# Keys' and values' block compression: two weight products of one 64-column half of the array each, one after the other or side by side

## The reference, cut to what matters

```python
def compress_blocks(t, w1, w2, pos):
    blk = t[:, idx] + pos[None, None, :, None, :]
    blk = jnp.moveaxis(blk, 3, 1).reshape(B, G, n_cmp, CMP_BLOCK * dh)
    return jax.nn.gelu(blk @ w1) @ w2
...
kc = compress_blocks(k_c, cmp_k_w1, cmp_k_w2, cmp_k_pos)
kc = rms_norm(kc, nsa_k_g)
vc = compress_blocks(v_c, cmp_v_w1, cmp_v_w2, cmp_v_pos)
```

## Time and profile before, and how to read it

| | us |
|---|---|
| median of 3 runs | 1147.88 |
| lowest and highest run | 1144.9, 1153.52 |
| the profiled execution | 1147.36 |
| its span (first to last instruction) | 1145.6 |
| its mean granted TensorE clock | 0.966 |

### The profile page before, as it was taken

One profiled execution on the slowest core, in us unless ns is written; L12 is line 12 of the kernel. 1 busy time (PEld: TensorE's weight loads), 2 busy tenths in 40 slices (PEclk: granted clock), 3 DMA queues, 4 the chain that ended last, 5 costly groups with the idle time before them and its releaser, 6 DMA issues.

```text
span 1145.6 us, 16492 instructions
## 1 busy us (share of the span) xinstructions
PE 1048.0 (91%) x6109; PEld 896.9 (78%) x6109; DVE 850.4 (74%) x1665; ACT 654.4 (57%) x1312; POOL 45.6 (4%) x44
## 2 busy tenths in 40 slices
PE   4898999896899999999988999799997999889997
PEld 4776878786687887888767989688875888878875
DVE  4677866674599999999968676697657877668674
ACT  5453645543688888887844576532445377642342
POOL 0201100000101001010000000000101000000010
PEclk9999999996899999999999999899998999889999
DMA  8432333341399999999944333332344433313320
GB/s 332 164 110 79 142 148 148 111 184 37 116 386 352 388 367 353 376 362 365 367 172 177 142 116 111 110 111 111 133 179 152 150 122 143 116 74 111 114 108 37
DMA packets 30036, 211.32 MB, mean 184 GB/s; under 512 B 3584, under 2 KB 3712, under 8 KB 4992
## 3 DMA queue, kind: packets, MB, share of 16 engines
q1 hardware_dynamic: 28368, 205.01, 48.3%
q10 hardware_dynamic: 1584, 5.20, 1.3%
HBM read 209.15 MB, written 1.05 MB: 183 GB/s over the span
## 4 chain that ended last, share of the span: by engine, by line
PE 52%; DVE 27%; DMA 9%; ACT 9%; issue 3%; POOL 0%; SPq 0%; DVEq 0%; POOLq 0%; ACTq 0%
DVE w_lo L398 13%; PE ps L507 12%; PE ps L509 12%; PE ps L508 12%; DMA ring<-in_panels 9%; PE ps L942 4%; PE ps L512 4%; ACT w_hi L1763 2%; PE ps L657 2%; PE ps L688 2%; ACT s_buf L1811 1%; PE ps L711 1%; DVE op_lo L398 1%; DVE scr L398 1%; DVE buf_d L1453 1%
## 5 line engine op out<-in xcount | busy, mean ns | idle before, releaser
L398 DVE TENSOR_TENSOR w_lo<-ring,w_hi 128x512 fp32r<-128x512 f32 x760 | 481.8, 689 | 129.6 <-ACT w_hi L1763 129.0
L1763 ACT ACTIVATE w_hi<-ring 128x512 fp32r<-128x512 f32 x760 | 425.0, 620 | 206.9 <-PE ps L509 166.6
L507 PE MATMUL ps<-w_hi,op_hi 128*128 128x512 f32 (+2 forms) x800 | 317.5, 397 | 21.1 <-ACT zin L1763 5.0
L509 PE MATMUL ps<-w_hi,op_lo 128*128 128x512 f32 (+2 forms) x800 | 309.9, 387 | 0.0
L508 PE MATMUL ps<-w_lo,op_hi 128*128 128x512 f32 (+2 forms) x800 | 309.5, 387 | 0.0
L507 PEld LDWEIGHTS ps<-w_hi,op_hi 128*128 128x128 f32 x800 | 152.5, 191 | 56.6 <-DVE w_lo L398 13.5
L509 PEld LDWEIGHTS ps<-w_hi,op_lo 128*128 128x128 f32 x800 | 151.9, 190 | 31.0
L508 PEld LDWEIGHTS ps<-w_lo,op_hi 128*128 128x128 f32 x800 | 152.7, 191 | 27.0
L507 PE MATMUL ps<-op_hi,w_hi 128*128 128x256 f32 x544 | 159.1, 292 | 4.2 <-DVE zin L1732 3.0
L508 PE MATMUL ps<-op_lo,w_hi 128*128 128x256 f32 x544 | 155.0, 285 | 0.0
L509 PE MATMUL ps<-op_hi,w_lo 128*128 128x256 f32 x544 | 154.8, 285 | 0.0
(11 more groups left out here) (243 smaller groups left out, 1129.0 us busy)
## 6 DMA issues: line engine op xcount, KB each, us to landing
ring<-in_panels SPq DMA_DIRECT2D x194, 1024.0 KB, 6.1
cst<-in_c ACTq DMA_DIRECT2D x1, 1219.0 KB, 5.4
buf_a<-in_pre ACTq DMA_DIRECT2D x2, 512.0 KB, 5.9
keys<-in_post ACTq DMA_DIRECT2D x2, 512.0 KB, 3.7
out<-x_tok SPq DMA_DIRECT2D x2, 512.0 KB, 2.6
cst<-in_c ACTq DMA_DIRECT2D x1, 960.0 KB, 6.1
x_tok<-in_x SPq DMA_DIRECT2D x1, 512.0 KB, 4.8
x_tok<-in_x ACTq DMA_DIRECT2D x1, 512.0 KB, 5.0
```

The costliest lines, as they stand in the source:

```text
L398: return V.tensor_tensor(o, a, b, op)
L507: T.matmul(o, l[0], r[0], start=start, stop=False)
L509: return T.matmul(o, l[1], r[0], start=False, stop=stop)
L1763: return A.activation(o, a, ACT.Copy, scale=scale)
```

## The change

Steps 3 and 4 no longer stand for keys and values but for the first and the second half of the 2048 rows. In each, keys' and values' matmuls alternate; keys go to PSUM partitions 0 to 63, values to 64 to 127, both in columns 0 to 255, so they use the two 64-column halves of the array. The raw halves are loaded in the order keys 0, values 0, keys 1, values 1. Gelu works on 128 x 256, step 5 is two full 128 x 128 transposes, and step 6 takes its operands from where these now lie. Waits and semaphores are unchanged.

```diff
             if n == 8 and h == 1:
-                out += [(2 * PN_CMP + i, 0, None) for i in range(2)]
+                out += [(2 * PN_CMP + i, 0, None) for i in (0, 2)]
             if n == 9 and h == 0:
-                out += [(2 * PN_CMP + 2 + i, 0, None) for i in range(2)]
+                out += [(2 * PN_CMP + i, 0, None) for i in (1, 3)]
...
                 elif step < 5:
-                    c = step - 3
+                    h = step - 3
                     pe.wait_ge(cmp_blk, 8)
-                    for h in range(2):
-                        load = raw_at[2 * c + h]
+                    w1 = []
+                    for load in raw_at[2 * h:2 * h + 2]:
                         pe.wait_ge(*landed(load))
...
-                        for n in range(8):
-                            m = T.matmul(ps[0:64, 7, c * 256:(c + 1) * 256], blk[c][:, 8 * h + n, :, :].rearrange("p g n -> p (g n)"),
-                                         w1[:, n, :], start=h == 0 and n == 0, stop=h == 1 and n == 7)
+                    for n in range(8):
+                        for c in range(2):
+                            m = T.matmul(ps[c * 64:(c + 1) * 64, 7, 0:256],
+                                         blk[c][:, 8 * h + n, :, :].rearrange("p g n -> p (g n)"),
+                                         w1[c][:, n, :], start=h == 0 and n == 0, stop=h == 1 and n == 7)
                 elif step == 5:
                     pe.wait_ge(cmp_a, 1)
-                    for i in range(4):
-                        m = turn128(ps[:, 7, i * 64:(i + 1) * 64], scr[0:64, i * P:(i + 1) * P], 64)
+                    for i in range(2):
+                        m = turn128(ps[:, 7, i * P:(i + 1) * P], scr[:, i * P:(i + 1) * P])
...
-                                         scr[:, 512 + (2 * c + i) * 64:512 + (2 * c + i + 1) * 64],
+                                         scr[:, 512 + (2 * i + c) * 64:512 + (2 * i + c + 1) * 64],
...
-                    A.activation(scr[0:64, 0:512], ps[0:64, 7, :], ACT.Gelu_apprx_tanh).then_inc(cmp_a, 1)
+                    A.activation(scr[:, 0:256], ps[:, 7, 0:256], ACT.Gelu_apprx_tanh).then_inc(cmp_a, 1)
```

More of the change, by code:

```diff
@@ L703, in compress @@
                 elif step < 5:
-                    c = step - 3
+                    h = step - 3
                     pe.wait_ge(cmp_blk, 8)
-                    for h in range(2):
-                        load = raw_at[2 * c + h]
+                    w1 = []
+                    for load in raw_at[2 * h:2 * h + 2]:
                         pe.wait_ge(*landed(load))
-                        w1 = ring[:, load % RING * HALF:(load % RING + 1) * HALF].rearrange("p (m n) -> p m n", m=8)
-                        for n in range(8):
-                            m = T.matmul(ps[0:64, 7, c * 256:(c + 1) * 256], blk[c][:, 8 * h + n, :, :].rearrange("p g n -> p (g n)"),
-                                         w1[:, n, :], start=h == 0 and n == 0, stop=h == 1 and n == 7)
+                        w1.append(ring[:, load % RING * HALF:(load % RING + 1) * HALF].rearrange("p (m n) -> p m n", m=8))
+                    for n in range(8):
[3 more added lines that the diff above has]
+                                         w1[c][:, n, :], start=h == 0 and n == 0, stop=h == 1 and n == 7)
                 elif step == 5:
                     pe.wait_ge(cmp_a, 1)
-                    for i in range(4):
-                        m = turn128(ps[:, 7, i * 64:(i + 1) * 64], scr[0:64, i * P:(i + 1) * P], 64)
+                    for i in range(2):
+                        m = turn128(ps[:, 7, i * P:(i + 1) * P], scr[:, i * P:(i + 1) * P])
                 elif step == 6:
```

## The result

The changed kernel takes 1140.06 us (median of 20 runs, 1134.53 to 1148.53) against 1149.13 us of the kernel before (20 runs, 1144.9 to 1155.5): a ratio of 0.9932, 95% interval 0.9912 to 0.9951. At 1149 us that is 7.8 us less, between 5.6 and 10.1. (The ratios of this document are not quotients of the medians: these two medians are 9.1 us apart.) The forecast was 1141.0 and 6.9 us less. The profiled execution took 1136.5 us, with a span of 1134.7.

The account below looks back on a forecast made before the run. TensorE was taken to bound the stage. Two steps saving 3.45 us each gave -6.90, with transposes, gelu and load order at 0: 1140.5 us from the profiled execution, 1141.0 for the median; range 1136.5 to 1147.

Parts of the forecast that it names:

- TensorE bounds the stage: Around steps 3 and 4 TensorE sets the end; a microsecond taken from L711's matmuls is one taken from the stage.
- A step costs 16 pitches and 0.14 us: Steps 3 and 4: records start in pairs 0.216 us apart, so each takes 3.60 us instead of 7.05.
- The rule quoted against the change: Rival, chance 0.04: each pair's weight load is not hidden under running matmuls; saving 2.5 us, time 1145.4 us.
- Transposes at 0: Step 5: two full transposes replace four records; counted 0, with -0.2 to +0.2 us as the ends.
- Gelu at 0: Gelu on half as many columns may save up to 0.3 us, but its result is read later; counted 0.
- the last of the three: Raw weight loads 21, 22 and 23, started between 158.9 and 159.9: the last lands at 170.3 at the latest.
- ACT's wait before gelu: Sign on ScalarE: its wait for the products of L711 falls from 6.0 to about 2.5 us.
- Nothing absorbed later: Behind steps 3 and 4 nothing hidden becomes late; the whole 6.90 us passes to the end; chance 0.72.
- no overlap: Rival for steps 3 and 4, chance 0.05: the halves do not run side by side, nothing saved, 1148 us.
- an emptied array: Rival, chance 0.03: each change of half in steps 3 and 4 empties the array; 4.5 us more, 1152.4 us.
- absorption: Rival, chance 0.13: waits and low clock behind step 6 take back 3 us of the gain; 1144 us.
- The clock: Moved TensorE gaps add or spare half-clock stretches, about 1.3 us each: 1137 to 1146 us; gain beyond 1% 0.03.

Follow-up runs that it names:

- the second profile: The changed kernel run and profiled again with no edit: 1140.55 us, ratio 0.9939 to the kernel before.
- the two with a gap of 1.17 and 0.86 us: Changed kernel with step 3 placed before the turn of take 31, 1140.48 us; changed kernel with steps 2 and 3 one take later, 1137.39 us.

## Why the prediction was right, point by point

- TensorE bounds the stage: right. Twice 3.45 us less of matmul became 6.94 us less between the turn and step 6.
- A step costs 16 pitches and 0.14 us: right, 3.60 us in the three full-clock steps of the changed kernel's two profiles. The reading of L688 carried it: same shape, same alternation, 0.80 us for what series would make 1.44.
- The rule quoted against the change, from TensorE: Matmul & The Clock Gate, Part 3, The mechanism, of the Trainium skill, would have made a step 5.79 us. The trace says 3.60, so loads into one column half do hide under matmuls of the other. The loads themselves overlap as well: the 33 of a changed step, 137 ns each at the median and so 4.5 us in sum, keep PEld busy for 2.20 us.
- Transposes at 0: right within 0.15 us. In the changed kernel 181.32 to 181.51 is 0.19 us against 0.33 before. But the transposes start 0.10 us later behind the scores, and the copy L1300 came 0.14 us later behind them: 1.34 us behind their start instead of 1.20. That passed on, as the prediction said that it would: the next turn waits 0.37 and 0.38 us for DVE in the changed kernel's two profiles and 0.19 in both of the kernel before. So 0.18 us of the 6.94 are given back behind step 6.
- Gelu at 0: it is 0.21 us shorter, and the table comes out without it.
- Loads: the last of the three was bounded by 170.3. ACT got it at 170.24 with step 3 slowed; in the second profile, with step 3 done at 159.27, its wait was the longest:

```profile
170.08 0.64 ACT L1765 ACTIVATE w_hi<-ring 128x512 fp32r<-128x512 f32 x1 [3.64 <-DMA ring<-in_panels]
174.51 1.28 ACT L1869 ACT_TABLE_LOAD   x1 [1.35 <-PE ps L712]
```

  That is ACT late by 3 us against the shifted plan, as the bound said. One forecast of the prediction was a little off by it: ACT's wait before gelu was put at about 2.5 us without counting that lateness, and was 1.35, so ACT was still 1.1 us late there. (In the first profile, where ACT was 1.5 us late at the load, it was 2.54.) This lateness reached no turn.
- Nothing absorbed later: right but for the 0.18 us above, by the last column of the table and the start of the expert stage. The rivals of no overlap, of an emptied array and of absorption fall.
- The clock: its worth per stretch was put at 1.3 us and is 1.65 where TensorE is busy throughout. The difference that it makes behind the stage, 955.4 against 950.1 us, was within the range given, and most of it arises where the prediction looked for it, in 265 to 296. It goes with the spread of the 20 runs over 14 us: the fastest, 1134.53 us, has a mean granted clock of 0.970 and the slowest, 1148.53, one of 0.958. Why the clock falls for 30.7 us on end in one execution and for less in another is not settled here.
- The number: that 1140.06 us lies within 1 us of 1141.0 is partly the draw. The medians are 9.1 us apart and the ratio gives 5.6 to 10.1, while the stages in the trace give 6.94; the mechanism rests on the trace, not on the closeness of the medians.

## What to carry to other kernels

Where two products each fill only 64 columns of the array, put their outputs into the two halves of the PSUM partitions and alternate them, singly or two by two; a shape with both already in the kernel's trace tells the price before anything is built. Placing them in two halves one behind the other gave 0.8 us a step here, of the 3.45 that alternation gave. When two profiles differ by more than the stage that changed, measure from a landmark behind the stage to the end in both, and take more than one profile of each kernel, before reading anything into the rest.

## What was not expected of the hardware

TensorE starts records of the other column half ahead of records that wait for their own half, but only about four places ahead of their turn (two float32 matmuls): sixteen matmuls in two blocks of eight took 6.24 us, in blocks of four 4.63, in blocks of two 3.66 and singly 3.60.

And a gap of 2.49 us in front of the same work was followed by a stretch at half clock in one profile of each kernel and not in the other, for 1.63 and 1.65 us. Over all profiles of this document in which the gap was 2.48 or 2.49 us, step 3 had such a stretch in five and none in three; in the two with a gap of 1.17 and 0.86 us it had none. Two are too few to say that a shorter gap keeps the clock up.
